# Attention probabilities transposed by VectorE in 32x32 blocks instead of by TensorE

## The reference

```python
s = jnp.einsum('bnqhgd,bnkhd->bnhgqk', qb, kb, ...) * (hd ** -0.5)
band_ok = (kj <= qi) & (kj > qi - WINDOW)
s = jnp.where(mask[None, :, None, None], s, NEG_INF)
m = jnp.maximum(jnp.max(s, axis=-1, keepdims=True), sink)
p = jnp.exp(s - m)
denom = jnp.sum(p, axis=-1, keepdims=True) + jnp.exp(sink - m)
o = jnp.einsum('bnhgqk,bnkhd->bnqhgd', (p / denom).astype(v.dtype), vb)
```

## Time and profile before

| what | value |
|---|---|
| median of 3 runs | 2123.92 us (2121.74 to 2124.45) |
| profiled execution, span from the first to the last instruction | 2121.0 us |
| TensorE busy in it | 2091.1 us, 99% |
| VectorE busy | 1512.2 us, 71% |
| ScalarE busy | 998.7 us, 47% |
| mean granted TensorE clock | 0.997 |

### The profile page before, as it was taken

The page is one execution under the profiler, slowest core; times in us unless marked ns, Lnnn a source line. Parts: engine busy times, 40 slices in busy tenths (PEclk is TensorE's granted clock), DMA queues, the critical chain, the costliest instruction groups (busy, mean ns, idle before and its releaser), DMA issues.

```text
span 2121.0 us, 24049 instructions
## 1 busy us (share of the span) xinstructions
PE 2091.1 (99%) x9575; PEld 1729.0 (82%) x9575; DVE 1512.2 (71%) x1724; ACT 998.7 (47%) x1257; POOL 4.6 (0%) x22
## 2 busy tenths in 40 slices
PE   7999999999999999999999999999999999999998
PEld 6788888888888878888888887888888888888887
DVE  6987987888788888886555889677555544555456
ACT  4577434443344455446555644554433444434444
POOL 0000000000000000000000000000000000000000
PEclk9999999999999999999999999999999999999999
DMA  9998998988899869975545678568655555555554
GB/s 354 387 383 301 330 324 322 327 327 283 306 337 327 284 218 328 322 243 171 160 161 161 238 285 309 200 232 307 211 183 191 193 185 198 179 198 196 183 177 159
DMA packets 249135, 539.70 MB, mean 254 GB/s; under 512 B 11584, under 2 KB 14016, under 8 KB 248384
## 3 DMA queue, kind: packets, MB, share of 16 engines
q1 hardware_dynamic: 248640, 538.04, 72.8%
q10 hardware_dynamic: 384, 0.13, 0.0%
HBM read 536.03 MB, written 2.10 MB: 254 GB/s over the span
## 4 chain that ended last, share of the span: by engine, by line
PE 92%; DVE 3%; DMA 1%; issue 1%; ACT 1%; SPq 1%; ACTq 0%; DVEq 0%
PE pa L639 15%; PE pa L642 15%; PE pa L641 15%; PE pb L639 14%; PE pb L642 14%; PE pb L641 14%; PE px L654 1%; DVE ada_acc L1572 1%; DMA raw<-in_ffn_w_in_dram 1%; DVE proj L2111 0%; ACT hi L1101 0%; DMA ada_s<-in_w_ada_dram 0%; DVE lo L1552 0%; PE px L722 0%; PE pm L981 0%
## 5 line engine op out<-in xcount | busy, mean ns | idle before, releaser
L1552 DVE TENSOR_TENSOR lo<-raw,hi 128x1024 fp32r<-128x1024 f32 (+1 forms) x732 | 868.9, 1196 | 526.9 <-ACT hi L1101 525.9
L1101 ACT CAST hi<-raw 128x1024 fp32r<-128x1024 f32 (+1 forms) x732 | 751.2, 1030 | 1005.5 <-PE pa L642 492.0
L639 PE MATMUL pa<-hi,act_hi 128*128 128x512 f32 (+1 forms) x1056 | 414.0, 392 | 7.6 <-DVE act_lo L1619 4.0
L642 PE MATMUL pa<-hi,act_lo 128*128 128x512 f32 (+1 forms) x1056 | 408.5, 387 | 0.0
L641 PE MATMUL pa<-lo,act_hi 128*128 128x512 f32 (+1 forms) x1056 | 408.1, 386 | 0.0
L639 PE MATMUL pb<-hi,act_hi 128*128 128x512 f32 x1024 | 403.2, 394 | 0.0
L642 PE MATMUL pb<-hi,act_lo 128*128 128x512 f32 x1024 | 398.8, 389 | 0.0
L641 PE MATMUL pb<-lo,act_hi 128*128 128x512 f32 x1024 | 398.6, 389 | 0.0
L1650 DVE SCALAR_TENSOR_TENSOR ada_acc<-ada_w,cond,ada_acc 128x1024 f32<-128x1024 f32 (+1 forms) x240 | 275.2, 1147 | 6.4 <-DVE ada_acc L1650 0.5
L639 PEld LDWEIGHTS pa<-hi,act_hi 128*128 128x128 f32 x1056 | 198.6, 188 | 51.8 <-DVE act_lo L1619 5.2
L642 PEld LDWEIGHTS pa<-hi,act_lo 128*128 128x128 f32 x1056 | 198.5, 188 | 40.8
(11 more groups left out here) (318 smaller groups left out, 1394.7 us busy)
## 6 DMA issues: line engine op xcount, KB each, us to landing
raw<-in_ffn_w_in_dram SPq DMA_DIRECT2D x176, 1024.0 KB, 5.1
ada_w<-in_w_ada_dram SPq DMA_DIRECT2D x224, 512.0 KB, 6.0
raw<-in_ffn_w_out_dram SPq DMA_DIRECT2D x64, 1024.0 KB, 5.1
raw<-in_w_in_dram SPq DMA_DIRECT2D x64, 1024.0 KB, 5.1
ada_s<-in_w_ada_dram SPq DMA_DIRECT2D x64, 512.0 KB, 10.4
raw<-in_ffn_w_out_dram SPq DMA_DIRECT2D x32, 768.0 KB, 4.5
raw<-in_w_out_dram SPq DMA_DIRECT2D x16, 1024.0 KB, 6.5
raw<-in_w_att_up_dram SPq DMA_DIRECT2D x8, 1024.0 KB, 5.1
```

Source lines behind the costliest of these rows:

```text
L639: pe.matmul(ps, a_hi[:, k0 + kk, tok], w_hi, start=start and kk == 0, stop=False, skip_group_check=on)
L642: mm = pe.matmul(ps, a_lo[:, k0 + kk, tok], w_hi, start=False, stop=stop and kk == n - 1, skip_group_check=on)
L1101: act.copy(hi_of(ph, i, j, half)[:, 0:n, 0:w], raw[:, j % RING, 2 * half:2 * half + n, 0:w])\
L1552: dve.tensor_tensor(lo[:, j % RING, s, 0:w], raw[:, j % RING, s, 0:w], hi_of(ph, i, j, half)[:, 0:n, 0:w].bitcast(F32), ALU.subtract)\
```

## The change

VectorE takes over the transposes. TensorE's `p_turn` and ScalarE's `pair_pt` go, with the semaphore `pt_mm`; VectorE gets a function `p_turn(n, tbs)` that transposes straight from `s_sb` to `p_t`, both in SBUF. VectorE's transpose works on 32x32 blocks, so each instruction takes 32 queries (`tb`, the input's partitions) and 32 keys (`fb`, the output's partitions) of both heads and of those of the three 128x128 blocks whose 32x32 block isn't emptied by the mask: all three on the diagonal (192 elements a partition), the two own blocks below it (128 elements), the earlier block above it (64 elements). The blocks left out stay zero in `p_t` from the first pair, n = 0, which transposes all (16 instructions of 192 elements). Each pair has 16 instructions. For an even pair, half of them stand behind `soft_b` at step 8 and half behind the `split` of step 9; for an odd pair all 16 stand at step 15 between the `split` and `soft_b`. `pt_ok` is now raised by the last of them. The transposes of pair n also wait for `o_mm` of pair n-1.

```diff
--- before.py
+++ after.py
@@ -352,7 +352,6 @@
         sc_mm = sem("sc_mm")
         mx_ok = sem("mx_ok")
         p_ok = sem("p_ok")
-        pt_mm = sem("pt_mm")
         pt_ok = sem("pt_ok")
         o_mm = sem("o_mm")
         o_ok = sem("o_ok")
@@ -982,13 +981,6 @@
                                        k_t[rows, (g + hh) % 2, 0:(tt + 1) * P], start=True, stop=True)
                 mm.then_inc(sc_mm, 1)
 
-            def p_turn(n):
-                pe.wait_ge(p_ok, n + 1)
-                for hh in (0, 1):
-                    for b in range(3):
-                        mm = pe.transpose(px[:, hh, b * P:(b + 1) * P], s_sb[:, hh, b * P:(b + 1) * P], ident[:, :])
-                mm.then_inc(pt_mm, 1)
-
             def values(n, g):
                 pe.wait_ge(pt_ok, n + 1)
                 for hh in (0, 1):
@@ -1021,8 +1013,6 @@
                     for b in range(3):
                         mm = pe.transpose(pr[:, b * P:(b + 1) * P], w_sb[:, b * P:(b + 1) * P], ident[:, :])
                     mm.then_inc(m_at, 1)
-                if n_ == 5:
-                    p_turn(2 * i)
                 if n_ == 7:
                     values(2 * i, g)
                     q_turn(2 * i + 1)
@@ -1036,8 +1026,6 @@
 
                     pe.wait_ge(m_h, i + 1)
                     scores(2 * i + 1)
-                if n_ == 13:
-                    p_turn(2 * i + 1)
                 if n_ == 15:
                     values(2 * i + 1, g)
                     if i == 3:
@@ -1449,11 +1437,6 @@
                                              bias=m_st[:, 4, o:o + 1], accum_out=m_st[:, 7, o:o + 1])
                 ins.then_inc(p_ok, 1)
 
-            def pair_pt(n):
-                act.wait_ge(pt_mm, n + 1)
-                act.copy(p_t[:, :, :, :], px[:, :, 0:3 * P].rearrange("p a (b t) -> p a b t", b=3))\
-                    .then_inc(pt_ok, 1)
-
             def heads_step(i, n_):
                 if n_ == 0:
                     act.wait_ge(m_qk, 1)
@@ -1473,8 +1456,6 @@
                 if n_ == 7:
                     act.wait_ge(m_at, i + 1)
                     act.copy(a_t[:, :, :], pr[:, 0:3 * P].rearrange("p (b t) -> p b t", b=3)).then_inc(m_atok, 1)
-                if n_ == 8:
-                    pair_pt(2 * i)
                 if n_ == 10:
                     pair_q(2 * i + 1)
                 if n_ == 12:
@@ -1489,8 +1470,6 @@
                 if (i, n_) == (3, 14):
                     act.wait_ge(m_var, 1)
                     act.activation(h_sq[:, 2, :, :], h_sq[:, 1, :, :], ACT.Sqrt).then_inc(m_rt, 1)
-                if n_ == 15:
-                    pair_pt(2 * i + 1)
                 if (i, n_) == (3, 15):
                     act.activation(proj[:, :, OO:OG], proj[:, :, OO:OG], ACT.Sigmoid).then_inc(proj_ok, 1)
 
@@ -2187,6 +2166,20 @@
                 link(dve.tensor_tensor(m_st[:, 7, :], m_st[:, 7, :], m_st[:, 6, :], ALU.add))
                 link(dve.reciprocal(m_st[:, 8, :], m_st[:, 7, :]))
 
+            def p_turn(n, tbs):
+
+                dve.wait_ge(p_ok, n + 1)
+                if n > 0:
+                    dve.wait_ge(o_mm, n)
+                for tb in tbs:
+                    for fb in range(4):
+                        turned = slice(0, 3) if n == 0 or tb == fb else slice(0, 3, 2) if tb > fb else slice(1, 2)
+                        src = s_sb[32 * tb:32 * (tb + 1), :, :].rearrange("p a (b k) -> p a b k", b=3)
+                        ins = dve.transpose(p_t[32 * fb:32 * (fb + 1), :, turned, 32 * tb:32 * (tb + 1)],
+                                            src[:, :, turned, 32 * fb:32 * (fb + 1)])
+                if tbs[-1] == 3:
+                    ins.then_inc(pt_ok, 1)
+
             def att_out(n):
                 dve.wait_ge(o_mm, n + 1)
                 for b in range(TT):
@@ -2234,6 +2227,9 @@
                     link(dve.reciprocal(m_st[:, 11, 2:4], m_st[:, 11, 0:2]))
                 if n_ == 8:
                     soft_b(i, 2 * i)
+                    p_turn(2 * i, (0, 1))
+                if n_ == 9:
+                    p_turn(2 * i, (2, 3))
                 if n_ == 10:
                     att_out(2 * i)
                 if n_ == 11:
@@ -2251,6 +2247,7 @@
                     dve.tensor_scalar(h_sq[:, 1, :, :], h_sq[:, 0, :, :], 1.0 / MV, EPS, ALU.mult, ALU.add)\
                         .then_inc(m_var, 1)
                 if n_ == 15:
+                    p_turn(2 * i + 1, (0, 1, 2, 3))
                     soft_b(i, 2 * i + 1)
                     if i == 3:
                         head_norms()
```

## The result

The kernel with the change takes 2147.54 us (median of 4 runs, 2147.30 to 2149.55) against 2123.11 us (median of 4, 2121.74 to 2124.45): ratio 1.0117, 95% interval 1.0104 to 1.0129. It is 24.4 us slower. Forecast were 16.8 us slower, 2140.7 us, with 2131 to 2151 as the range; the measured time lies in this range, but above the 2137 to 2145 that the prediction gave to its own case. The profiled executions differ by the same amount, 2145.6 against 2121.0 us.

A forecast was written before the change was run, and what follows sets the result against it. The prediction took TensorE, busy 99% of 2121.0 us, as the bound. Transposes -5.3, waits at step 7 +17.0, last boundary +2.7 and clock +2.4 gave +16.8 us: 2123.9 to 2140.7 us, range 2131 to 2151.

The forecast's parts named there:

- its own case: Whole kernel: the forecast of 16.8 us slower, covering 2137 to 2145 us from 0 to 4 clock falls; chance 0.70.
- dearer case: Rival: short strided transposes each cost 0.1 us more, with waits at step 15 too; +31, 2155 us; chance 0.12.
- TensorE's transposes: TensorE's queue: eight sets of six transposes, 0.66 us each, leave the path, 5.3 us won.
- The length of a short transpose: VectorE: 377, 310 and 243 ns for 192, 128 and 64 elements, each held until earlier ones finish; 4.99 us a pair.
- Waits at step 7: TensorE waits for `p_t` before `values`: 5.2 us in iteration 0, 3.95 in each of three others; sum 17.0.
- Step 15 free in iterations 0 to 2: Odd pairs' transposes at step 15 fit with 0.34 us to spare, so TensorE doesn't wait there.
- Last boundary: End of iteration 3 into `up`: 2.7 us in all, 1.2 of it a wait at `values`.
- Clock: TensorE at half clock behind two of the four new gaps, 1.2 us each, 2.4 us; bounds 0 and 4.8.
- The rule on idle gaps: Trainium skill on TensorE's gaps between bursts of matmuls: clock falls at all four, 4.8 us in place of 2.4.
- Overlap: Rival: VectorE's transposes overlap by 0.08 us each, gaps of 2.5 at step 7, no clock fall; +7.2, 2131 us; chance 0.10.
- not slower: Rival: VectorE's fixed part isn't paid in a run of transposes; +0.8, 2124.7 us; chance 0.04.

The follow-up runs named there:

- e4: Against the changed kernel, even pairs are transposed at step 6 and odd pairs at step 14; 2117.81 us, ratio 0.9974 to the kernel before.
- e7: Against the changed kernel, each transpose is divided by head, 32 a pair in place of 16, at the same places; 2150.79 us.
- e1: Against the changed kernel, all 16 transposes of an even pair stand at step 8, ahead of the split of unit 9; 2139.69 us.
- e2: Changed kernel plus useless TensorE matmuls before `values` at step 7, 20 in iteration 0 and 15 in the others; 2135.60 us.
- e3: Against the changed kernel, even pairs go back to TensorE and ScalarE, odd pairs stay on VectorE at step 15; 2122.69 us.
- e5: Changed kernel plus useless TensorE matmuls before `values` at step 7, only 14 in iteration 0 and 9 in the others; 2137.07 us.

## Why the prediction was right, and where its size was off

The direction and the mechanism held; the forecast was 7.6 us too low. The measured 2147.5 us lies inside the range of 2131 to 2151 only because the range was drawn wide enough to take in part of the dearer case; by the prediction's own sum, with all four falls, 2145 was the most. Term by term the clock is 7.7 too low, the stretch ahead of the heads 1.4 (it was put at nothing), the waits at step 7 are 1.2 too high and the last boundary 0.2. Step by step:

- **TensorE's transposes, -5.3.** Held. e4 shows it bare: 5.48 less in the heads.
- **The length of a short transpose.** Worked out 377, 310, 243 ns; measured 369, 302, 237. Halves 2.36 and 2.63; measured 2.31 and 2.59. The slope of other VectorE instructions carried over within 3%. That each is held until the last one ends was right: 0.01 between them. The Trainium skill's rule in "VectorE: DVE Perf Modes", section "Two Vector instructions with no wait between them", holds an instruction whose output starts in another quarter; the trace agrees on both sides: no overlap where the quarter changes, and one of 0.056 us where it doesn't (e7).
- **Waits at step 7, +17.0.** 15.85. The relay was as read: the `split` of unit 9 stands between the halves. What I had too long was the step from the last transpose to the first matmul, 0.3 us; measured 0.05 (1061.29 + 2.59 = 1063.88 to 1063.93). The 0.2 in it for a weight load was too much, but there is such a load: `values` gives `p_t` as the stationary operand (the first input of `pe.matmul`), and it is this load that waits.

```profile
1063.93 0.50 PEld L988 LDWEIGHTS pm<-proj,p_t 128*128 128x128 f32 x2 [3.93 <-DVE p_t L2178]
```

  The profile starts the waiting matmul together with its load, so the load shows behind that start: in e1 the first two matmuls take 0.27 us until L990 follows (1060.12 to 1060.39), without a gap 0.16 (1034.73 to 1034.89). This 0.1 us, some 0.4 for four waits, is not in the 15.85 but in what I put down to the clock; e2, which took 9.8 of the 10.1 away, leaves about this much over.
- **Step 15 free in iterations 0 to 2.** Held, as in e3; e7 shows that the slack is as small as said.
- **Last boundary, +2.7.** 2.5, first at `values`, then at the first unit of `up`, as forecast.
- **Clock, +2.4.** This is the term that was mis-sized: 10.1. Two things in it were wrong. I took two falls of four, and there were four, which alone would have given 4.8. And, the larger part, I took 1.2 us for each from the earlier trace rows, where about half of the low stretch (3.1 of 6.8 us) lay inside the idle gap and cost nothing, and only 2.9 over the matmuls behind it; here 3.4 to 6.1 us of each lie over working matmuls. The measured value lies outside my bounds of 0 to 4.8: at 2.5 us a fall costs twice what I took. With full clock in the heads (e2) the changed kernel would have come to 2135.6, close to the forecast without its clock term, 2138.3.
- **The rule on idle gaps.** The Trainium skill ("TensorE: Matmul & The Clock Gate", section "Why this matters for your kernels") counted all four falls, and the trace agrees: gaps of 3.5 to 4.7 us, four falls. The gaps of which it warns are longer than the 2.25 us that were enough in e1; there the measurement decides.
- **Rivals.** Overlap (gaps of 2.5) and not slower fell with the durations above; so did dearer transposes, at 237 to 369 ns and no gap at step 15. The sum of 24.4 lay nearer to the dearer case (+31) than to mine by time alone; only the gaps in the trace tell that it is the clock and not the transposes.
- **Ahead of the heads, +1.38.** Not foreseen, and not the change's doing as far as the runs tell: about 1.2 of it is the fall behind the 2.00 us gap at 785.

Left open: what decides whether the clock falls behind a gap of 2.00 us (six of ten times it did), and why the low stretch lasts 3.4 us at one place and 6.8 at another. Of the 10 us, e2 shows the sum over the four; how it divides among them (about 1.7 in iteration 0 and 2.6 to 3.0 in each other one) is worked out from the lengths of the iterations. Half of the low stretch over working matmuls, 1.7, 2.7, 3.0 and 3.1, comes to nearly the same. Reckoned so, the fall at 785 would cost 1.7, and the trace shows about 1.2.

## What to carry to other kernels

Whether another engine can take work over is not told by its idle share (89 of 201 us here) but by where it is idle in its own order, beside the moment when the result is wanted. Put the taken-over work where its input is ready and ahead of the next link of the relay: the same 16 instructions, two steps earlier for the even pairs and one for the odd, turned 24 us of loss into 5 us of gain. And price a new gap on TensorE twice, once for its length and once for the matmuls behind it that run at half clock; here the second price was two thirds of the gaps' length in the changed kernel (10.1 for 15.2 us) and nine tenths in e1 (9.3 for 10.2), so that it falls little when the gap gets shorter, until the gap brings no fall at all.

## What the runs showed of the hardware

- The granted clock of TensorE in this kernel: no fall behind any gap of 0.7 to 1.70 us between dense matmuls (1.70 at the last boundary of e7, 1.46 to 1.54 in e5), a fall in six of ten executions behind one of 1.99 to 2.00, and a fall at every one of the twelve from 2.25 to 5.66 us (changed kernel, e1, e7). Half clock then lasts 3.4 or 6.8 us.
- The fall comes late: in the changed kernel 2.1 to 2.8 us into the idle time in iterations 1 to 3, and in iteration 0 only at 1008.0, 0.6 us past the end of the gap, so that it lay wholly over working matmuls. In e1 it came 0.4 to 1.4 us past the end of the three gaps of 2.25 us.
- A transpose of VectorE on 32 partitions in fp32 takes 182, 215 (mean), 237, 302 and 369 ns for 32, 64, 64, 128 and 192 elements. The two for 64 elements differ in form: 237 are two heads of 32, 215 is one head with two blocks.
- From the end of the last transpose to the recorded start of the weight load and matmul that wait for it: 0.05 us; the load then adds about 0.1 us to the first matmul (e1).
